# A first stage of one pass over tiles, rewritten as two passes over pairs of tiles by Strassen's form

## The chip, the cores and the metric

The kernel runs on one core of one Trainium2 chip. The metric is the device time of one execution in microseconds (us); lower is better. TensorE is called PE below, VectorE DVE, ScalarE ACT, GpSimd POOL, and SyncE, which here only issues DMAs, SP.

## What is computed

One layer of a transformer-like block on 2048 positions of width 1024, all float32:

```python
h = rms_norm(x, norm_mix_pre)
z = h @ w_in                      # 1024 -> q 512 | k 128 | v 128 | u 512 | v 512
q, k = apply_rope(q), apply_rope(k)
a_out = window_sink_attention(q, k, v, attn_sinks)   # 8 heads, 2 kv heads, chunks of 64
g_in = gelu(z[..., o3:])
s_out = spatial_gating(g_in[..., :512], g_in[..., 512:], ...)  # layer norm, 128x128 per group
mix = concat([rms_norm(a_out), rms_norm(s_out)]) @ w_out
x = x + rms_norm(mix)
x = x + rms_norm(swiglu(rms_norm(x), w_gate, w_up, w_down))
```

The change concerns the first product (`h @ w_in`) and what hangs on it: the gate branch (u, v, gelu, spatial gating), and q, k, v with the attention.

## The kernel before

A float32 product is made of three fast ones: each operand is split into a rounded part `_hi` (a copy on ACT, type fp32r) and a rest `_lo` (a subtraction on DVE), and `three` issues hi\*hi, hi\*lo and lo\*hi. The gain of the pre-norm is multiplied into the weights while they are split; the row factor `rstdx` is applied when the result is read.

There are four stages. **Stage one** loops over 16 tiles of 128 positions. For each, PE makes q, k, v into `ZA` (`z_qkv`: 24 matmuls of 512 columns and 24 of 256) and u, v of the gate branch into `ZB` (`z_columns`, 48 matmuls of 512 columns), plain products over 8 chunks of 128. Between them stand, in an order that is written out by hand, the transposes of q and k, the scores, the transposes of the probabilities, the spatial product (`sgu_w`) and the weighted sum of the values. The products for tile k+1 are issued while ACT and DVE do the softmax of tile k, so PE always has a long product between two short steps that wait. The result `mix` goes to DRAM (`mix_d`). **Stage two** (`tile2`) reads it back, multiplies by `w_out` (48 matmuls a tile), adds the residual, norms and stores. Its first two products begin in the last tile of stage one. **Stage three** (gate and up of the SwiGLU) and **stage four** (down) already use Strassen's form: of a 2x2 block product 7 block products are made in place of 8. For that the left and the right operand each need four sums, and the result needs chains of sums. In stage three `t_sums` on POOL makes the sums of the weights, `t_hi_parts` on ACT and `t_lo_parts` on DVE split them in three instructions, `copies` on ACT brings products 1 and 2 from PSUM, `chain`, `upper` and `lower` on DVE and `corner` on POOL put the quarters of the result together. Stages three and four are not touched.

Each engine works through its own list in order; a `wait_ge` at the head of a list holds everything behind it on that engine. All DMAs are issued by SP, also in order.

Of the kernel before, what the change touches and what calls it, by code (L numbers as in the profile page):

```python
# [5 lines left out]
F32 = mybir.dt.float32  # L6
# [6 lines left out]
P = 128  # L13
# [6 lines left out]
SW = 512  # L20
# [14 lines left out]
RAWS = 6  # L35
# [10 lines left out]
def build_kernel(nc, x, x_t, w_in, w_out, w_gu, w_dn, gain_in, gain_out, post_mix, pre_ffn,  # L46
                 post_ffn, sinks, ln_g, ln_b, sgu_wt, sgu_bt, rope, out):
    mix_d = nc.dram_tensor("mix_d", (SEQ, D), F32).ap()
    x1_d = nc.dram_tensor("x1_d", (SEQ, D), F32).ap()
# [12 lines left out]
    wq_hi = at("wq_hi", 90, [KD, QKV], F32R)  # L62
    wq_lo = at("wq_lo", 114, [KD, QKV], F32R)
    wg_hi = at("wg_hi", 138, [KD, 2 * SW], F32R)
    wg_lo = at("wg_lo", 170, [KD, 2 * SW], F32R)
    wraw = [at(f"wraw{i}", 10 + 4 * i if i < 4 else 48 + 4 * i, [2 * SW]) for i in range(RAWS)]
    ropeA = at("ropeA", 0, [AW + P])
    ropeB = at("ropeB", 2.5, [AW + P])
    qT = at("qT", 5, [AW])
    kA = [at(f"kA{i}", 7 + 0.5 * i, [P]) for i in range(2)]  # L70
    kB = at("kB", 8, [P])
    vA = [at(f"vA{i}", 8.5 + 0.5 * i, [P]) for i in range(2)]
    vB = at("vB", 9.5, [P])
    probs = at("probs", 10, [NH * P])
    probsT = at("probsT", 14, [NH * P])
    gel = at("gel", 18, [2 * SW])
    vhat = at("vhat", 22, [SW])
    vn1 = at("vn1", 24, [SW])
    vn = at("vn", 26, [SW])
    sB = at("sB", 28, [SW])  # L80
    aO = at("aO", 30, [AW])
    hT_hi = [at(f"hT_hi{i}", 32 + 4 * i, [D], F32R) for i in range(2)]
    hT_raw = [at(f"hT_raw{i}", 40 + 4 * i, [D]) for i in range(2)]
    hT_lo = [at(f"hT_lo{i}", 40 + 4 * i, [D], F32R) for i in range(2)]
    xt = [at(f"xt{i}", 48 + 4 * i, [D]) for i in range(2)]
    qrot = at("qrot", 60, [AW])
    krot = at("krot", 62, [P])
    mix = [at(f"mix{i}", 64 + 4 * i, [D]) for i in range(2)]
    cs = at("cs", 72, [TILES, 96])
    lng = at("lng", 78, [SW])  # L90
    lnb = at("lnb", 80, [SW])
    squares1 = at("squares1", 82, [D], BF16)


    wout_raw = [at(f"wout_raw{c}", 88 + 4 * c, [D]) for c in range(KD)]
    wout_hi = at("wout_hi", 120, [KD, D], F32R)
    wout_lo = at("wout_lo", 152, [KD, D], F32R)
# [48 lines left out]
    gcol_in, gcol_out = small("gcol_in", KD), small("gcol_out", KD)  # L146
# [3 lines left out]
    ssx, msx, rstdx = small("ssx", 2), small("msx", 2), small("rstdx", 2)  # L150
# [3 lines left out]
    st6, mv, varm, rstdv = small("st6", 6), small("mv", 2), small("varm", 1), small("rstdv", 1)  # L154
    ss2, ms2, rs2 = small("ss2", 2), small("ms2", 2), small("rs2", 2)
# [14 lines left out]
    DN = [T0[:, :], T1[:, :]]  # L170

# [8 lines left out]
    wraw_in = [sem(f"wraw_in{i}") for i in range(RAWS)]  # L180
    win_hi_done, win_split = sem("win_hi_done"), sem("win_split")
    x_in, hT_in, mix_out = pair("x_in"), pair("hT_in"), pair("mix_out")
    id_zero, pool_consts = sem("id_zero"), sem("pool_consts")
    ssx_done, msx_ready, rstdx_ready = sem("ssx_done"), sem("msx_ready"), sem("rstdx_ready")
    t_full, t_drained = pair("t_full"), pair("t_drained")
    h_hi_done, h_split, zqkv_full, zus_full = sem("h_hi_done"), sem("h_split"), sem("zqkv_full"), sem("zus_full")
    rope_mul, rot_done, v_done, k_done = sem("rope_mul"), sem("rot_done"), sem("v_done"), sem("k_done")
    gel_done, st6_done, mv_done, var_ready = sem("gel_done"), sem("st6_done"), sem("mv_done"), sem("var_ready")
    rstdv_ready, vhat_done, vn1_done, vn_ready = sem("rstdv_ready"), sem("vhat_done"), sem("vn1_done"), sem("vn_ready")
    s_full, masked, mraw_done = sem("s_full"), sem("masked"), sem("mraw_done")  # L190
    mtop_done, soft_ready, exp_done = sem("mtop_done"), sem("soft_ready"), sem("exp_done")
    dtot_done, rden_done, g_full, pv_done = sem("dtot_done"), sem("rden_done"), sem("g_full"), sem("pv_done")
    sB_done, aO_done, ss2_done, ms2_ready = sem("sB_done"), sem("aO_done"), sem("ss2_done"), sem("ms2_ready")
    rs2_ready, mix_done = sem("rs2_ready"), sem("mix_done")
# [47 lines left out]
    def use_q(k):  # L242
        return 2 * k

    def use_p(k):
        return 2 * k + 1

    def over_tiles(e, body):

        body(0, 0, 0, 0, True)
        body(0, 1, 1, 0, True)
        with e.Fori(1, TILES // 2 - 1) as j:
            for par in range(2):
# [12 lines left out]
    PIECES = [(c, wq_hi, wq_lo, slice(0, QKV)) for c in range(KD)] + \  # L268
             [(c, wg_hi, wg_lo, slice(QKV, WIN)) for c in range(KD)]

    def piece(i):
        c, hi, lo, w = PIECES[i]
        return c, w, wraw[i % RAWS][:, 0:w.stop - w.start], hi[:, c, :], lo[:, c, :]

    block = nc.Block()
    with block:

        @block.sync
        def _(e):
            e.dma_start(hT_raw[0][:, :], x_t[0, :, :]).then_inc(hT_in[0], 16)  # L280
            e.dma_start(gcol_in[:, :], gain_in).then_inc(gains_in, 16)
            for i in range(len(PIECES)):
                c, w, raw, hi, lo = piece(i)
                if i >= RAWS:
                    e.wait_ge(win_split, i + 1 - RAWS)
                e.dma_start(raw, w_in[chunk(c), w]).then_inc(wraw_in[i % RAWS], 16)
                if i == 3:
                    for m in range(2):
                        e.dma_start(xt[m][:, :], x[m * P:(m + 1) * P, :]).then_inc(x_in[m], 16)
                    e.dma_start(hT_raw[1][:, :], x_t[1, :, :]).then_inc(hT_in[1], 16)  # L290
                    e.dma_start(cs[:, 0:1, :], rope[:, 0:1, :]).then_inc(cs_in, 16)
            for dst, src in ((cs[:, 1:TILES, :], rope[:, 1:TILES, :]), (sgu_w[:, :, :], sgu_wt)):
                e.dma_start(dst, src).then_inc(consts, 16)
            for dst, src in ((sgub, sgu_bt), (sinkb, sinks), (lng, ln_g), (lnb, ln_b), (gcol_out, gain_out)):
                e.dma_start(dst[:, :], src).then_inc(consts, 16)
            for m in (2, 3):
                e.wait_ge(ssx_done, m - 1)
                e.dma_start(xt[m % 2][:, :], x[m * P:(m + 1) * P, :]).then_inc(x_in[m % 2], 16)

            def tile(k, par, more, ahead=True):  # L300
                if more:
                    e.wait_ge(ssx_done, k + 3)
                    e.dma_start(xt[par][:, :], x[rows(k + 4), :]).then_inc(x_in[par], 16)
                if ahead:
                    e.wait_ge(zus_full, k + 1)
                    e.dma_start(hT_raw[par][:, :], x_t[bass.ds(k + 2, 1), :, :].rearrange("t p n -> (t p) n"))\
                        .then_inc(hT_in[par], 16)
                e.wait_ge(mix_done, 2 * k + 2)
                e.dma_start(mix_d[rows(k), :], mix[par][:, :]).then_inc(mix_out[par], 16)

            with e.Fori(0, TILES // 2 - 2) as j:
                for par in range(2):
                    tile(j * 2 + par, par, True)
            for k in range(TILES - 4, TILES - 2):
                tile(k, k % 2, False)


            e.wait_ge(zqkv_full, TILES)
            for c in range(KD):
                e.dma_start(wout_raw[c][:, :], w_out[chunk(c), :]).then_inc(wout_in[c], 16)  # L320
            for p in range(2):
                e.wait_ge(mix_out[p], 16 * (TILES // 2 - 1))
                e.dma_start(mixin[p][:, :], mix_d[p * P:(p + 1) * P, :]).then_inc(mix_in[p], 16)
            tile(TILES - 2, 0, False, False)
            e.wait_ge(zus_full, TILES)
            for p in range(2):
                e.wait_ge(rot_done, 2 * TILES)
                e.wait_ge(t_full[1], use_q(TILES - 1) + 1)
                e.dma_start(xres[p][:, :], x[p * P:(p + 1) * P, :]).then_inc(xres_in[p], 16)
            e.dma_start(postm[:, :], post_mix).then_inc(posts, 16)  # L330
# [5 lines left out]
            def load_mix(k, par):  # L336
                e.wait_ge(mixT_full, 2 * k - 2)
                e.dma_start(mixin[par][:, :], mix_d[rows(k), :]).then_inc(mix_in[par], 16)
# [1139 lines left out]
```

## Time and profile before

| | us |
|---|---|
| median of 3 runs | 1917.43 (1917.12 to 1918.08) |
| profiled execution | 1919.53 |
| its span in the profile | 1917.7 |
| first matmul | 8.84 |
| gate product of the first tile starts | 23.31 |
| gate product of the last tile starts | 393.30 |
| first two products with `w_out` done | 441.46 |

The profiled execution is 2.1 us above the median; 1.8 us of it lie outside the span. The last line of the table is the end of stage one for this document: from there on both kernels do the same. A row of a timeline gives start, duration, engine, line and operation; the durations of matmuls overlap, so their pace is read from their starts.

### The profile page before, as it was taken

What the parts mean: (1) busy time and instruction counts of PE and PEld (TensorE: products, weight loads), DVE (VectorE), ACT (ScalarE), POOL (GpSimd) and SP (SyncE); (2) the same over time, 40 slices, a digit from 0 to 9 for tenths busy, and PEclk for the clock granted to TensorE, in tenths of its full rate; (3) what the DMA queues carried; (4) which work ended last, traced back from release to release, by engine and by line L of the source; (5) the groups of instructions that cost most, each with busy time, mean ns of one, the idle gap of its engine ahead of it and who ended that gap; (6) DMA issues with size and microseconds to landing.
All of it is one profiled execution on the core that took longest, in us unless ns stands there. A gap on an engine that the chain in (4) does not pass through costs nothing. (4 is left out here: it accounts for less than half of the span.)

```text
span 1917.7 us, 25255 instructions
## 1 busy us (share of the span) xinstructions
PE 1866.2 (97%) x9464; PEld 1545.9 (81%) x9464; DVE 1178.6 (61%) x1286; ACT 711.6 (37%) x1169; POOL 560.8 (29%) x406
## 2 busy tenths in 40 slices
PE   7999999989999899999999899999999899999998
PEld 5888888878888788888888688888887788888886
DVE  5444444464546877677767867677767546554564
ACT  6555555453335432323234333323333122222342
POOL 2222222220002444444444444444442000000243
PEclk9999999999999999999999999999999999999999
DMA  7111111044574434233326333233324853445665
GB/s 274 67 66 66 66 66 55 33 179 178 206 275 183 171 103 130 87 104 98 126 82 221 119 108 117 82 104 116 108 82 151 335 212 126 174 167 187 228 206 180
DMA packets 128966, 270.26 MB, mean 141 GB/s; under 512 B 5920, under 2 KB 84768, under 8 KB 119456
## 3 DMA queue, kind: packets, MB, share of 16 engines
q1 hardware_dynamic: 128928, 269.78, 40.3%
q8 instruction: 21, 0.34, 0.1%
q14 instruction: 17, 0.14, 0.0%
HBM read 189.54 MB, written 80.22 MB: 141 GB/s over the span
## 5 line engine op out<-in xcount | busy, mean ns | idle before, releaser
L1220 PE MATMUL T<-tb_hi,sb_hi 128*128 128x512 f32 x616 | 240.9, 391 | 7.1 <-DVE sb_lo L1133 7.1
L1221 PE MATMUL T<-tb_lo,sb_hi 128*128 128x512 f32 x616 | 240.2, 390 | 0.0
L1222 PE MATMUL T<-tb_hi,sb_lo 128*128 128x512 f32 x616 | 240.2, 390 | 0.0
L1018 DVE TENSOR_TENSOR t_lo<-t_raw,t_hi 128x1536 fp32r<-128x1536 f32 x132 | 223.8, 1749 | 0.0
L807 ACT ACTIVATE sb_hi<-sb_raw 128x1408 fp32r<-128x1408 f32 x56 | 77.4, 1381 | 299.1 <-PE T L1222 259.5
L571 POOL TENSOR_TENSOR v<-u,p 128x512 f32<-128x512 f32 x44 | 116.2, 2640 | 183.4 <-DVE u L1042 158.3
L1397 PE MATMUL T<-s_hi,t_hi 128*128 128x512 f32 x352 | 138.6, 394 | 6.4 <-DVE s_lo L1011 4.5
L555 POOL TENSOR_TENSOR t_raw<-t_raw 128x512 f32<-128x512 f32 x44 | 60.8, 1381 | 281.1 <-DMA t_raw<-w_gu 281.1
L1220 PEld LDWEIGHTS T<-tb_hi,sb_hi 128*128 128x128 f32 x616 | 116.0, 188 | 32.9 <-issue 8.2
L1399 PE MATMUL T<-s_hi,t_lo 128*128 128x512 f32 x352 | 138.4, 393 | 0.0
L1398 PE MATMUL T<-s_lo,t_hi 128*128 128x512 f32 x352 | 138.0, 392 | 0.0
L1397 PE MATMUL ZB<-s_hi,t_hi 128*128 128x512 f32 x352 | 136.9, 389 | 0.0
L1398 PE MATMUL ZB<-s_lo,t_hi 128*128 128x512 f32 x352 | 136.9, 389 | 0.0
L1399 PE MATMUL ZB<-s_hi,t_lo 128*128 128x512 f32 x352 | 136.9, 389 | 0.0
L1221 PEld LDWEIGHTS T<-tb_lo,sb_hi 128*128 128x128 f32 x616 | 116.1, 188 | 24.2
L1222 PEld LDWEIGHTS T<-tb_hi,sb_lo 128*128 128x128 f32 x616 | 115.9, 188 | 24.1
L1133 DVE TENSOR_TENSOR sb_lo<-sb_raw,sb_hi 128x1408 fp32r<-128x1408 f32 x56 | 96.2, 1718 | 51.5 <-ACT sb_hi L807 51.5
L756 ACT ACTIVATE th<-v 128x512 f32<-128x512 f32 x66 | 41.7, 632 | 218.1 <-POOL v L571 120.0
L595 POOL TENSOR_TENSOR rstdf<-msf,mhalf 128x1 f32<-128x1 f32 x16 | 14.5, 906 | 359.9 <-ACT msf L816 359.9
L1397 PE MATMUL ZA<-s_hi,t_hi 128*128 128x512 f32 x264 | 104.6, 396 | 4.9 <-DVE u L1042 2.7
L1220 PE MATMUL ZB<-wg_hi,hT_hi 128*128 128x512 f32 x256 | 103.1, 403 | 1.6 <-DVE wg_lo L967 1.6
L1398 PE MATMUL ZA<-s_lo,t_hi 128*128 128x512 f32 x264 | 104.1, 394 | 0.0
(194 smaller groups left out, 4522.4 us busy)
## 6 DMA issues: line engine op xcount, KB each, us to landing
t_raw<-w_gu SPq DMA_DIRECT2D x44, 1024.0 KB, 4.8
act_d<-ac SPq DMA_DIRECT2D x22, 1792.0 KB, 8.0
sb_raw<-act_d SPq DMA_DIRECT2D x56, 704.0 KB, 4.1
h_d<-quarters SPq DMA_DIRECT2D x8, 1792.0 KB, 6.6
s_raw<-h_d SPq DMA_DIRECT2D x14, 1024.0 KB, 8.1
tb_raw<-w_dn SPq DMA_DIRECT2D x6, 1536.0 KB, 6.3
hT_raw<-x_t SPq DMA_DIRECT2D x16, 512.0 KB, 3.2
xt<-x SPq DMA_DIRECT2D x16, 512.0 KB, 3.9
```

Of the source, the lines that this page charges most:

```text
L555: e.tensor_tensor(t[:, R3, :], t[:, B22, :], t[:, B12, :], ALU.subtract).then_inc(tsum_done, 1)
L571: e.tensor_tensor(v22[:, :], u3[:, :], p5[:, :], ALU.add).then_inc(v22_done, 1)
L756: e.activation(th[i][:, :], src, ACT.Tanh, scale=0.5).then_inc(th_done, 1)
L807: e.activation(sb_hi[it % 2][:, :, :], sb_raw[it % 2][:, :, :], ACT.Copy).then_inc(sb_hi_done, 1)
L1018: e.tensor_tensor(t_lo[u][:, first:end, :], t_raw[u][:, first:end, :], t_hi[u][:, first - 1:end - 1, :].bitcast(F32), ALU.subtract).then_i ...
L1133: e.tensor_tensor(sb_lo[it % 2][:, :, :], sb_raw[it % 2][:, :, :], sb_hi[it % 2][:, :, :].bitcast(F32), ALU.subtract).then_inc(sb_split, 1)
L1220: e.matmul(out_ap, lhi, rhi, start=start, stop=False)
L1221: e.matmul(out_ap, lhi, rlo, start=False, stop=False)
L1222: return e.matmul(out_ap, llo, rhi, start=False, stop=stop)
L1397: e.matmul(bank, hi, s_hi[i][:, :, w], start=i < 4 and k == 0, stop=False, skip_group_check=True)
L1398: e.matmul(bank, hi, s_lo[i][:, :, w], start=False, stop=False, skip_group_check=True)
L1399: ins = e.matmul(bank, lo, s_hi[i][:, :, w], start=False, stop=k == HK - 1, skip_group_check=True)
```

## The change

Stage one becomes two passes over 8 pairs of tiles. The first goes from the last pair (j = 0) to the first one (j = 7) and does the gate branch; the second goes from the first pair (p = 0) to the last and does q, k, v with the attention. Both use Strassen's form over the pair: 7 products of 12 matmuls, of 512 columns in pass one (`uv_product`) and of 384 in pass two (`qkv_product`).

The left operand comes as four quarters of x (`x_q`, 1024 KB a pair). DVE multiplies them by the gain (`scale_xq`, 128x2048), POOL makes four sums (`left_sums`), ACT and DVE split the seven operands (`left_hi`, `left_lo`). They are stored to DRAM (`hl_d`, twice 1792 KB a pair) and loaded again by pass two (`load_hl`). The right operands (weights) are summed and split once per pass: for pass one at the start, for pass two in the last iteration of pass one. The chains of sums are those of stage three, on DVE (`uv_u2`, `uv_u3`, `uv_upper`, `uv_lower`) and POOL (`bv22`). The normed half of the gate branch now goes through two instructions on DVE (`tn`, `vn`) where DVE made one and POOL two. Gelu no longer alternates with Exp on ACT. The first two products with `w_out` are spread between the attention steps of the last three tiles.

The diff, cut to its core:

```diff
+            def left_sums(j):
+                q = lb_raw[j % 2]
+                e.wait_ge(xq_scaled, j + 1)
+                e.tensor_tensor(q[:, 4, :], q[:, 0, :], q[:, 3, :], ALU.add).then_inc(lsum_done, 1)
+                e.wait_ge(lsum_done, 4 * j + 1)
+                e.tensor_tensor(q[:, 5, :], q[:, 4, :], q[:, 1, :], ALU.subtract).then_inc(lsum_done, 1)
+                e.tensor_tensor(q[:, 6, :], q[:, 1, :], q[:, 0, :], ALU.subtract).then_inc(lsum_done, 1)
+                e.wait_ge(lsum_done, 4 * j + 2)
+                e.tensor_tensor(q[:, 7, :], q[:, 2, :], q[:, 5, :], ALU.subtract).then_inc(lsum_done, 1)
...
+                if j + 1 == NP:
+                    e.wait_ge(w_in_loaded[B12], 32)
+                    e.wait_ge(w_in_loaded[B22], 32)
+                    e.wait_ge(in_done, 7 * j + 4)
+                    e.tensor_tensor(wq_raw[3][:, :, :], wq_in[:, B22, :, :], wq_in[:, B12, :, :],
+                                    ALU.subtract).then_inc(w_sum3, 1)
...
+            for j in range(NP):
+                ahead = j + 1 < NP
+                uv_copy(j, 0)
...
+                if ahead:
+                    stats_x(j + 1)
+                    left_hi(j + 1, 1)
+                    left_hi(j + 1, 2)
+                else:
+                    for i in range(1, 5):
+                        wq_hi_part(i)
+                gelus(j)
...
+            def left_lo(j, c):
+                b = j % 2
+                first, end = ((1, 4), (4, 6), (6, 8))[c]
+                if c == 0:
+                    e.wait_ge(lsum_done, 4 * j + 4)
...
+                if ahead:
+                    scale_xq(j + 1)
+                else:
+                    wq_lo_part(0)
+                if j:
+                    gate(j - 1, 0)
+                if ahead:
+                    left_lo(j + 1, 0)
+                else:
+                    wq_sum(R1)
+                uv_u2(j)
...
+                uv_u3(j)
+                if ahead:
+                    left_lo(j + 1, 1)
+                    left_lo(j + 1, 2)
+                norm_stats(j, 1)
+                normed(j, 1)
...
+                uv_upper(j)
+                norm_stats(j, 0)
+                uv_lower(j)
...
+                normed(j, 0)
...
+            def uv_product(j, i):
...
+                if i in (4, 5):
+                    e.wait_ge(in_copied, 2 * j + i - 3)
+                if i == 6:
+                    e.wait_ge(u3_first, j + 1)
...
+            def spatial(j, par):
+                n = 2 * j + 1 - par
...
+                e.wait_ge(vn_ready, n + 1)
+                if par:
+                    e.wait_ge(v21_first, j + 1)
...
+            for j in range(NP):
+                for i in range(7):
+                    uv_product(j, i)
+                    if j and i < 2:
+                        spatial(j - 1, 1 - i)
...
+            e.wait_ge(w_split, 7 + 7)
+            load_hl(1)
```

`in_done` counts products, `u3_first`, `v12_first`, `v21_first`, `v22_first` the parts of the result (`bu3`, `bv12`, `bv21`, `bv22`), `vn_ready` the normed halves, `w_split` the split weights, `lsum_done` the sums on POOL.

DVE, one tile of the kernel before, inside its loop (`hT_lo` is the split of the left operand, `st`, `mv`, `varm`, `vhat` the layer norm, `sB` the gate's result, `mix` what is stored):

```order
L851 TENSOR_TENSOR hT_lo_81<-hT_raw_79,hT_hi_77 128x1024
...
L904 BN_STATS st_191<-gel 128x6
L907 BN_AGGR mv<-st_191 128x2
L909 TENSOR_SCALAR varm<-mv 128x1
L913 TENSOR_SCALAR vhat<-gel,mv,rstdv 128x512
...
L934 SCALAR_TENSOR_TENSOR sB<-S,sgub,gel 128x128 x4
...
L945 TENSOR_SCALAR mix_87<-sB,rs_197 128x512
```

DVE, one iteration of pass one in the changed kernel (`lb_raw` the quarters and sums of the left operand, `lb_lo` their rests, `bu`, `bv` the chain, `tn`, `vn` the norm; the two halves of the norm read alike, the first is shown whole):

```order
L1123 SCALAR_TENSOR_TENSOR sB_94<-ZA,sgub,gu_88 128x128 x4
L1077 TENSOR_TENSOR lb_raw_70<-lb_raw_70,gq 128x2048
L1123 SCALAR_TENSOR_TENSOR sB_93<-ZA,sgub,gu_87 128x128 x4
L1087 TENSOR_TENSOR lb_lo_72<-lb_raw_70,lb_hi_74 128x1536
L1159 TENSOR_TENSOR bu_82<-S,bp_80 128x512
L1131 TENSOR_SCALAR sB_94<-sB_94,rsB 128x512
L1131 TENSOR_SCALAR sB_93<-sB_93,rsB 128x512
L1166 TENSOR_TENSOR bu_83<-S,bu_82 128x512
L1087 TENSOR_TENSOR lb_lo_72<-lb_raw_70,lb_hi_74 128x1024 x2
L1137 BN_STATS st_261<-bv_86 128x6
L1139 BN_AGGR mv<-st_261 128x2
L1141 TENSOR_SCALAR varm<-mv 128x1
```

The list went from one split of 1024 elements a tile to a scaling of 2048 and splits of 3584 a pair, with four sums of PSUM banks, and the split of the next pair stands ahead of this pair's `bu_83`.

POOL, the same iteration in the changed kernel (`rsB`, `rstdx`, `rstdv` are powers of a column or two, `bv_86` is `bv22`):

```order
L529 TENSOR_TENSOR lb_raw_70<-lb_raw_70 128x512
L531 TENSOR_TENSOR lb_raw_70<-lb_raw_70 128x512
L532 TENSOR_TENSOR lb_raw_70<-lb_raw_70 128x512
L534 TENSOR_TENSOR lb_raw_70<-lb_raw_70 128x512
L524 TENSOR_TENSOR rsB<-msB,mhalf 128x2
L524 TENSOR_TENSOR rstdx<-msx,mhalf 128x2
L565 TENSOR_TENSOR bv_86<-bu_83,bp_81 128x512
L524 TENSOR_TENSOR rstdv<-varm,mhalf 128x1 x2
```

All of these are new there but the powers; the sums of the next pair stand ahead of this pair's `bv_86`.

DVE at the start of the changed kernel, up to the first weights (`wu_b` and `wu_raw` are loaded or summed weights, `wu_lo` their rests):

```order
L1077 TENSOR_TENSOR lb_raw_70<-lb_raw_70,gq 128x2048
L1096 TENSOR_TENSOR wu_lo_56<-wu_b_97,wu_hi_63 128x2048
L1103 TENSOR_TENSOR wu_raw_50<-wu_b_98,wu_b_97 128x2048
L1107 TENSOR_TENSOR wu_raw_51<-wu_raw_54,wu_raw_50 128x2048
L1087 TENSOR_TENSOR lb_lo_72<-lb_raw_70,lb_hi_74 128x1536
```

Before the first product stood one split of `hT_raw` (1024 elements) and one of 768 elements; now the scaling, a split and two sums of 2048 each and a split of 1536 stand there.

## Rows read from the trace of the kernel before

**Rows 1.** The page: span, and busy time of each engine
```profile
span 1917.7 us, 25255 instructions
PE 1866.2 (97%) x9464; PEld 1545.9 (81%) x9464; DVE 1178.6 (61%) x1286; ACT 711.6 (37%) x1169; POOL 560.8 (29%) x406
```

**Rows 2.** Windows: a start, tiles 1 to 14, a cold stretch; busy, clock, DMA
```profile
8.00:12.00 4.00, 3.16 (x9) 2.72 (x10) 3.60 (x4) 2.37 (x3) 0.00 (x0) 1.00 1.03 417
...
44.00:393.40 349.40, 348.19 (x2610) 292.50 (x2608) 166.30 (x356) 176.71 (x478) 90.40 (x99) 1.00 0.17 59
...
1076.00:1080.00 4.00, 3.91 (x10) 3.17 (x11) 4.00 (x3) 1.12 (x2) 2.66 (x1) 0.57 1.03 291
```

**Rows 3.** Timeline of PE: the first matmul, one tile, the last tile's start
```profile
8.84 0.77 PE L1220 MATMUL ZA<-wq_hi,hT_hi 128*128 128x512 f32 x1 [8.84 <-DVE wq_lo L967]
...
202.77 0.39 PE L1222 MATMUL ZB<-wg_hi,hT_lo 128*128 128x512 f32 x1
...
203.65 0.47 PE L1220 MATMUL ZB<-wg_hi,hT_hi 128*128 128x512 f32 x1
...
208.99 0.39 PE L1222 MATMUL ZB<-wg_hi,hT_lo 128*128 128x512 f32 x1
...
210.34 0.50 PE L1220 MATMUL ZA<-wq_hi,hT_hi 128*128 128x512 f32 x1
...
216.07 0.28 PE L1221 MATMUL ZA<-wq_lo,hT_hi 128*128 128x256 f32 x1
...
218.71 0.28 PE L1222 MATMUL ZA<-wq_hi,hT_lo 128*128 128x256 f32 x1
218.83 1.04 PE L1313 MATMUL T<-ident,probs 128*128 128x128 f32 x8
219.70 1.06 PE L1320 MATMUL S<-vn,sgu_w 128*128 128x128 f32 x8
220.84 0.27 PE L1329 MATMUL S<-vA,probsT 128*64 128x64 f32 x1
...
221.92 0.50 PE L1220 MATMUL ZB<-wg_hi,hT_hi 128*128 128x512 f32 x1
...
393.30 0.50 PE L1220 MATMUL ZB<-wg_hi,hT_hi 128*128 128x512 f32 x1
...
441.46 0.71 PE L1347 MATMUL S<-ident,h2n 128*128 128x128 f32 x5
```

**Rows 4.** Timeline of ACT: product 1 of two neighbouring halves in stage three
```profile
902.35 0.60 ACT L749 ACTIVATE p<-T 128x512 f32<-128x512 f32 x1 [12.45 <-PE T L1399]
...
921.39 0.60 ACT L749 ACTIVATE p<-ZB 128x512 f32<-128x512 f32 x1 [0.39 <-PE ZB L1399]
```

**Rows 5.** Timeline of DVE: wide subtractions, without and with POOL beside them
```profile
614.55 4.49 DVE L1011 TENSOR_TENSOR s_lo<-s_raw,s_hi 128x2048 fp32r<-128x2048 f32 x2
618.96 4.02 DVE L1018 TENSOR_TENSOR t_lo<-t_raw,t_hi 128x1536 fp32r<-128x1536 f32 x3
...
911.28 5.11 DVE L1018 TENSOR_TENSOR t_lo<-t_raw,t_hi 128x1536 fp32r<-128x1536 f32 x3
```

**Rows 6.** Timeline of POOL: the corner beside them, and one of the four sums
```profile
911.59 2.58 POOL L571 TENSOR_TENSOR v<-u,p 128x512 f32<-128x512 f32 x1 [3.40 <-DVE u L1042]
...
1038.13 1.29 POOL L558 TENSOR_TENSOR t_raw<-t_raw 128x512 f32<-128x512 f32 x1
```

**Rows 7.** Timeline of DVE: the layer norm and the gate's result
```profile
212.09 0.69 DVE L904 BATCH_NORM_STATS2 st<-gel 128x6 f32<-128x512 f32 x1
...
213.16 0.15 DVE L909 TENSOR_SCALAR varm<-mv 128x1 f32<-128x1 f32 x1
...
222.22 1.12 DVE L934 SCALAR_TENSOR_TENSOR sB<-S,sgub,gel 128x128 f32<-128x128 f32 x4
```

**Rows 8.** DMA issues: KB each, median us from issue to landing
```profile
t_raw<-w_gu SPq DMA_DIRECT2D x44, 1024.0 KB, 4.8
...
h_d<-quarters SPq DMA_DIRECT2D x8, 1792.0 KB, 6.6
```

More of the change, by code:

```diff
@@ L84, in build_kernel @@
[L84 to L96, printed above, removed]
@@ L300, in tile @@
[L300 to L309, printed above, removed]
@@ L311, in _ @@
[L311 to L323, printed above, removed]
@@ L871, in rope_products, with keys @@
                                            op0=ALU.mult, op1=ALU.mult).then_inc(rope_mul, 1)
-            def tile(j, par, before, last, ahead):
-                k = 2 * j + par
-                if not last:
-                    h_lo(k + 1, 1 - par)
-                e.wait_ge(t_full[1], use_q(k) + 1)
+            def keys(k):
+                par = k % 2
+                e.wait_ge(k_full, k + 1)
+                if k:
+                    e.wait_ge(s_full, k)
                 e.tensor_copy(kB[:, :], T1[:, 0:P]).then_inc(k_done, 1)
@@ new lines, in spatial @@
+            def spatial(j, par):
+                n = 2 * j + 1 - par
+                if n == 0:
+                    e.wait_ge(pool_consts, 4)
+                e.wait_ge(vn_ready, n + 1)
+                if par:
+                    e.wait_ge(v21_first, j + 1)
+                bank = GU[j % 2][2 + par]
+                for g in range(SG):
+                    ins = e.matmul(bank[:, chunk(g)], sgu_w[:, g, :], vn[par][:, chunk(g)], start=True, stop=True)
+                ins.then_inc(g_full, 1)
@@ L1295, in tile @@
                 for i in range(PAIRS):
-                    for half, keys in enumerate((kA[par], kB)):
+                    for half, window in enumerate((kA[k % 2], kB)):
                         for kv in range(KVH):
@@ new lines, in out_units @@
+            def out_units(k, first, end):
+                par = k % 2
+                if first == 0:
+                    e.wait_ge(mixT_split, 2 * k + 2)
+                    if k == 0:
+                        e.wait_ge(z11_done, NP)
+                        e.wait_ge(v12_first, NP + NP)
+                    if k == 1:
+                        e.wait_ge(u2_first, NP + NP)
+                        e.wait_ge(v21_first, NP + NP)
+                    if k >= 2:
+                        e.wait_ge(y_done, k - 1)
+                for unit in range(first, end):
+                    c, a = unit // 2, unit % 2
+                    w = slice(a * 512, (a + 1) * 512)
+                    if k == 0 and a == 0:
+                        e.wait_ge(wout_split, c + 1)
+                    ins = three(M[par][:, a, :], mixT_hi[par][:, chunk(c)], mixT_lo[par][:, chunk(c)],
+                                wout_hi[c][:, w], wout_lo[c][:, w], c == 0, c == KD - 1)
+                if end == 2 * KD:
+                    ins.then_inc(mm2_full, 1)
@@ new lines, in _ @@
+            for i in range(7):
+                qkv_product(0, i)
+                if i < 2:
+                    spatial(NP - 1, 1 - i)
+            for j in range(NP - 1):
+                p = j + 1
+                qkv_product(p, 0)
+                turn_qk(2 * j)
+                if j:
+                    turn_probs(2 * j - 1)
+                qkv_product(p, 1, range(0, 2))
+                scores(2 * j)
+                qkv_product(p, 1, range(2, 4))
+                qkv_product(p, 2)
+                if j:
+                    weighted(2 * j - 1)
+                qkv_product(p, 3)
+                turn_qk(2 * j + 1)
+                qkv_product(p, 4, range(0, 2))
+                turn_probs(2 * j)
+                qkv_product(p, 4, range(2, 4))
+                scores(2 * j + 1)
+                if p == NP - 1:
+                    mix_transposes(0)
+                qkv_product(p, 5)
+                qkv_product(p, 6)
+                weighted(2 * j)
@@ new lines, in _ @@
+            out_units(0, 0, 3)
+            turn_qk(TILES - 2)
+            turn_probs(TILES - 3)
+            out_units(0, 3, 5)
+            scores(TILES - 2)
+            out_units(0, 5, 9)
+            weighted(TILES - 3)
+            out_units(0, 9, 12)
+            turn_qk(TILES - 1)
+            out_units(0, 12, 16)
+            mix_transposes(1)
+            turn_probs(TILES - 2)
+            out_units(1, 0, 2)
+            scores(TILES - 1)
+            weighted(TILES - 2)
+            out_units(1, 2, 11)
```

1336 lines of the change are left out of this document (869 added, 467 removed).

## The prediction

> **What bounds the kernel now.** I read the page first: PE is busy for 97% of the span [rows 1], so only what shortens PE's list, or makes it wait, can move the time. Then the windows: from 44 to 393 us, fourteen tiles, PE is busy for 348.19 of 349.40 us, while DVE works 166, ACT 177 and POOL 90 of them [rows 2]. Stage one is bound by PE, and the others have slack of half their time. The timeline of PE gives its prices. A matmul of 512 columns takes 0.2267 us: two neighbouring halves of stage three, 84 matmuls each, start 19.04 apart [rows 4]. One of 256 takes 0.120 (22 of them from 216.07 to 218.71). A tile takes (393.30-221.92)/7 = 24.48; less 72 x 0.2267 and 24 x 0.120 this leaves 5.28 for its small steps: transposes of q and k (203.65-202.77, less one matmul, 0.65), scores (1.12), transposes of the probabilities (0.87), spatial product (1.14), weighted sum (1.08), and some 0.4 for the switches [rows 3]. Stage one with the two first products of `w_out` ends at 441.46. Its content on PE is 16 x 24.48 + 96 x 0.2267 + 3 for the transposes of `mix` = 416.5; so 25 us are waits, 8.84 of them ahead of the first matmul.
>
> **What PE's list saves.** Pass one, a pair: 84 x 0.2267 = 19.04, and two spatial products at 1.14 + 0.2 for the switch: 21.7. Pass two, a pair: 84 matmuls of 384 columns, a size that the trace doesn't have; between 0.120 and 0.2267 I take the middle, 0.1733, which makes 14.56 (bounds 10.1 and 19.0; the two paces lie on a line through nearly zero, so the middle is good to some hundredths). With it go the small steps of two tiles without the spatial ones, 2 x 4.14, and some 0.5 for two more switches: 23.3. In all 8 x 21.7 + 8 x 23.3 + 24.8 = 385. The list is 31 us shorter. The Trainium skill (TensorE: Matmul & The Clock Gate, "Wait — 56ns, not 53.3ns?") gives a warm matmul its columns at 2.4 GHz and about 2.5 ns; by that 384 columns would take 0.1625 and pass two would be 7 us shorter in all. The rows at 512 columns lie 5% above what it gives, so the sum stays with the rows.
>
> **What DVE and POOL get: the steady pair of pass one.** Here the gain is lost. Prices on DVE, start to start: 0.61 for 512 elements, 1.13 for 1024, 1.67 for 1536 (4.02 for the three parts of a split), 2.2 for 2048 (4.49 for two) [rows 5], 1.05 for the four parts of the gate's result, 1.22 from `bn_stats` to the end of `varm` [rows 7]. A sum of 512 on POOL takes 1.29 and its four follow one another in 5.4 [rows 6]. And the two engines exclude each other when both have two inputs in SBUF: the same split takes 4.02 alone and 5.11 with the corner beside it, which takes 2.58 in place of 1.29 [rows 5, 6].
>
> I walk once through DVE's list from y, the moment at which `uv_lower` of the pair before is done. PE has waited for it (`v21_first`), and makes the spatial product: the gate's first half can start at y+1.45 (the second half of the norm fits before it) and ends at y+2.5. Scaling, 2.2: y+4.7. Only now can POOL begin the sums, done at y+10.2; DVE makes the second gate (1.05) and then stands for 4.4 us, since `left_lo` wants all four sums. Split of 1536: y+11.9. `uv_u2` 0.61, and two products with `rsB` (0.8), which wait for POOL's two powers, themselves locked out by that split (some 0.6): y+13.9. `uv_u3`: y+14.5. The two splits of 1024 with the corner between them: 1.13 + 1.3 + 1.13, y+18.1. The norm's first half: 1.22 + 0.61, some 0.6 for the power on POOL behind it, 0.61: y+21.1. `uv_upper` 0.61, 0.8 for the gelu that it feeds on ACT, second half of the norm 1.83, `uv_lower` 0.61: y+25.0, and some 0.3 for semaphores. The loop is **25.3**, against PE's 21.7: PE stands 3.6 us in each pair, in front of the spatial product. So pass one is DVE's, with DVE busy for only 17. Bounds: 22.8 if no lock cost anything, 27 if each met twice. The loads don't set it: `x_q` is issued as the pair before ends and lands 4.8 later [rows 8], before its scaling.
>
> **The start.** Loads run at 417 GB/s [rows 2], so a megabyte lands every 2.5 to 3 us: `x_q` near 5.8, the quarters of the weights near 8.6, 11.4, 14.2 and 17. DVE has scaling, seven splits and three sums of 2048 and a split of the left operand in three parts: 11 x 2.2 + 4 = 28 us, and the lock adds a sum on POOL of four times 1.29 (5.2) and one of 1.3; it starts at 5.9 and waits 3.5 for the first rounded weights. The first matmul starts near 26.7 in place of 8.84 [rows 3], the weights are done at 44. Product 7 waits for `uv_u3`, behind the scaling (2.2), the sums (5.4), a split (1.67) and two sums of the next pair: 54.5. The first pair ends at **57.2**. Its `uv_lower` comes 10.5 after `uv_u3`, so y is 7.9 for the second pair, which takes 7.9 + 19.2 = **27.1**; pairs 3 to 7 take 5 x 25.3 = **126.5**.
>
> **From pass one to pass two.** In the last iteration the weights of pass two take the place of the left splits. Counted from its start: `uv_u3` at 22, the corner at 23.3, then on POOL a difference of 1536 (three times 1.29, 3.9): 27.2. ACT's list has the rounding of this and of the next weight (1.5 each) ahead of all gelus, so the norm can start only at 31; with two splits of 1536 in between, `uv_lower` ends near 40. PE is through with the pair at 25, has one product of pass two (2.1) to do, and stands 12 us in front of the spatial product. The rest of that pair of products ends near 55. The next one needs `hl_d`, whose load waits for the last split of the weights (near 50; it lands where `wq_in` lay): twice 1792 KB, 11 us at 417 GB/s with the landing (13.2 if they ran one after the other at 6.6 [rows 8]). It starts near **62.5**; its content would have been 39.
>
> **Pass two and the end.** A tile's chain through the scores (scores 1.1, maxima 1.7, exponentials 2.9, transposes 0.9, copy 0.7, semaphores) is under 8 us and comes twice in 23.3; DVE has some 15, ACT 14 and POOL 6 us of work. I charge nothing, and the cover is the seven products: 21.1 for the pair that has no tile behind it, 6 x 23.4, and a transposition: **162.6**. The end: 96 matmuls, the small steps of two and a half tiles, transposes of `mix`, and 1 for waits: **35.5**.
>
> **The sum.** 57.2 + 27.1 + 126.5 + 62.5 + 162.6 + 35.5 = 471.4 in place of 441.5: 30 longer. Seen otherwise: 31 less on PE, 61 more in waits (start about 23, pass one 23, the passage 23, less what stood at the old end). The later stages are the same. The profiled span of 1917.7 becomes 1948; the median lies 0.3 below the span: **1947**. From one measurement to the next this kernel differs by less than 0.2%, 3.8 us, which I take as the bound of "same".
>
> **Rivals.**
> *The queues as walked* (0.62): 1935 to 1960. The parts are good to 1 us a pair in pass one (7), 4 each at the start and the passage, 1 a pair in pass two.
> *Some of the waits don't come* (0.18): DVE's order bites less than I walk, say 22.8 a pair for want of locks (-18 over seven pairs) and some of the passage: 1916 to 1933. For it speaks that in stage three the same chain leaves PE without waits; against it, that there the sums on POOL are made long before DVE wants them, here never.
> *PE stays the bound* (0.12), the rival on the other side: if a pair costs DVE less than 21.7 and the passage is covered, the 31 us come back in full: 1886, and half of them with the start as walked, 1903. It decides at 21.7; DVE's own work is 17, and the 4.4 for the sums would have to vanish. The order of DVE's list speaks against it: nothing stands between the second gate and the split.
> *It is worse* (0.08): each wait of PE is followed by a cold stretch (clock 0.57 in a window after such a wait [rows 2]), which DVE's loop hides in pass one but nothing hides at the start and in the passage; or pass two waits 2 us a pair for a list on ACT or DVE: 1962 to 1975.
>
> **How the numbers follow.** The first case gives 1947. From 1920 to 1963 lie all of it and most of the second, some 8 in 10; its own range is 1935 to 1960. Faster, below 1913.6: the third case, 0.12. Same: 0.06, out of the second. Slower: 0.82.
>
> **What would show it.** In the profile after: first matmul near 27; starts of product 1 in pass one 25 us apart, with PE idle 3 to 4 us released by DVE's `bv` (line 1176) ahead of the spatial product; DVE idle 4 to 5 us a pair released by POOL (line 534) ahead of line 1087; a wait of 12 us at the passage and one of 7 released by the DMA of `hl_d`; starts in pass two 23.4 apart. I am wrong if pairs of pass one are 22 us apart, or if ACT makes its gelus ahead of the weights.

## The result, and the profile after

The changed kernel takes 1966.05 us (median of 4 runs, 1964.69 to 1970.17), the kernel before 1917.76 in the same comparison: ratio 1.0251, 95% interval 1.0239 to 1.0264. It is slower, as forecast, and 3 us above the upper end of the range of 1920 to 1963.

The page of the changed kernel, to be held against [rows 1]. Its profiled execution took 1964.88 us.

```profile
span 1963.0 us, 24683 instructions
...
PE 1841.8 (94%) x9272; PEld 1538.7 (78%) x9272; DVE 1273.7 (65%) x1386; ACT 714.2 (36%) x1201; POOL 605.7 (31%) x424
```

PE has 24 us less to do, and the span is 45.3 longer: the saving is there, and some 70 us of waits eat it. The timeline of PE gives the borders of the parts of the sum; in brackets stands the idle time before the row, and what ended it.

```profile
26.35 0.77 PE L1696 MATMUL T<-wu_hi,lb_hi 128*128 128x512 f32 x1 [26.35 <-DVE lb_lo L1087]
...
48.28 0.77 PE L1696 MATMUL T<-wu_hi,lb_hi 128*128 128x512 f32 x1 [5.15 <-ACT bp L713]
...
59.81 0.63 PE L1696 MATMUL ZB<-wu_hi,lb_hi 128*128 128x512 f32 x1
...
65.62 1.13 PE L1710 MATMUL ZA<-vn,sgu_w 128*128 128x128 f32 x8 [2.65 <-DVE bv L1176]
...
83.88 0.39 PE L1696 MATMUL T<-wu_hi,lb_hi 128*128 128x512 f32 x1
...
91.23 2.05 PE L1710 MATMUL S<-vn,sgu_w 128*128 128x128 f32 x8 [4.47 <-DVE bv L1176]
...
212.19 0.39 PE L1696 MATMUL ZB<-wu_hi,lb_hi 128*128 128x512 f32 x1
...
217.06 1.75 PE L1710 MATMUL ZA<-vn,sgu_w 128*128 128x128 f32 x8 [1.99 <-DVE bv L1176]
...
250.80 2.04 PE L1710 MATMUL S<-vn,sgu_w 128*128 128x128 f32 x8 [11.61 <-DVE bv L1176]
...
273.79 0.69 PE L1745 MATMUL ZA<-wq_hi,lb_hi 128*128 128x384 f32 x1 [6.52 <-DMA lb_lo<-hl_d]
...
435.77 0.47 PE L1669 MATMUL ZA<-wout_hi,mixT_hi 128*128 128x512 f32 x1 [1.55 <-DVE z L1269]
...
444.00 1.08 PE L1759 MATMUL T<-ident,qrot 128*128 128x128 f32 x4 [5.92 <-issue]
...
488.30 1.04 PE L1896 MATMUL S<-ident,h2n 128*128 128x128 f32 x8
```

Each term of the forecast sum beside what these rows give (the pairs start at 59.81, 83.88 and, the last of pass one, 212.19):

| part | forecast | measured |
|---|---|---|
| first pair | 57.2 | 59.8 |
| second pair | 27.1 | 24.1 |
| pairs 3 to 7 | 126.5 | 128.3 |
| last of pass one to second pair of pass two | 62.5 | 61.6 |
| pass two | 162.6 | 162.0 |
| end, up to the first transposes of stage two | 35.5 | **52.5** |
| sum | 471.4 | 488.3 |

Five of six terms are good to 3 us and cancel; the end is 17.0 us too short, the whole miss of 16.9 at this border. The waits inside it, beside the one of 5.92 above:

```profile
454.01 0.50 PE L1669 MATMUL ZA<-wout_hi,mixT_hi 128*128 128x512 f32 x1 [1.13 <-DVE wout_lo L1351]
...
460.51 0.50 PE L1669 MATMUL ZA<-wout_hi,mixT_hi 128*128 128x512 f32 x1 [1.64 <-DVE wout_lo L1351]
...
463.10 0.50 PE L1669 MATMUL ZA<-wout_hi,mixT_hi 128*128 128x512 f32 x1 [0.92 <-DVE wout_lo L1351]
...
469.19 0.50 PE L1669 MATMUL ZB<-wout_hi,mixT_hi 128*128 128x512 f32 x1 [2.69 <-DVE mixT_lo L1359]
...
484.17 0.24 PE L1800 MATMUL T<-vA,probsT 128*64 128x64 f32 x1 [1.08 <-ACT probsT L837]
```

What follows the border takes 1474.7 us, before 1476.2 (1917.7 less 441.46). The windows of the end show both halves of its excess, idle PE and a low clock (columns as in [rows 2]):

```profile
444.00:452.00 8.00, 8.00 (x57) 6.55 (x58) 4.54 (x11) 4.17 (x9) 2.24 (x3) 0.66 0.00 1
...
468.00:476.00 8.00, 6.81 (x77) 5.26 (x78) 3.59 (x7) 1.67 (x8) 0.55 (x1) 0.79 0.90 310
...
435.00:488.00 53.00, 38.86 (x304) 30.44 (x305) 27.88 (x51) 27.40 (x88) 6.67 (x10) 0.90 0.24 80
```

The longest wait of the end, 5.92 us ahead of the turn of q and k of tile 14, is one for several semaphores, and the profile writes "issue" where it names none. The timeline of DVE shows what was late:

```profile
439.15 1.28 DVE L1351 SCALAR_TENSOR_TENSOR wout_lo<-wout_raw,gcol_out,wout_hi 128x1024 fp32r<-128x1024 f32 x1 [1.27 <-ACT wout_hi L852]
442.01 1.28 DVE L1351 SCALAR_TENSOR_TENSOR wout_lo<-wout_raw,gcol_out,wout_hi 128x1024 fp32r<-128x1024 f32 x1 [1.58 <-ACT wout_hi L852]
443.21 0.68 DVE L1338 TENSOR_TENSOR aO<-T,rden 128x512 f32<-128x512 f32 x1
```

and that of ACT why:

```profile
437.93 1.18 ACT L852 ACTIVATE wout_hi<-wout_raw,gcol_out 128x1024 fp32r<-128x1024 f32 x1
440.83 1.15 ACT L852 ACTIVATE wout_hi<-wout_raw,gcol_out 128x1024 fp32r<-128x1024 f32 x1 [1.71 <-DVE wout_lo L1351]
```

The turn (the transposes of q and k) overwrites the bank from which DVE still has to read the output of tile 12 (`aO`, 443.21; it ends at 443.89, and the turn starts at 444.00). That reading stands in DVE's list behind two splits of `w_out`, these behind ACT's, the first of ACT's behind eight exponentials, and the second waits for DVE's first, since an odd part waits for the split before it. A relay of four steps lies ahead of an instruction of 0.7 us.

### The profile page after: what moved, and what is told of

Its sections match the earlier page's. It is cut to its first block and busy times, and to the rows that moved or that the text cites. A ratio compares the mean times of both kernels' runs of the same rounds, so it can differ in the third digit from the quotient of the medians.

```text
span 1963.0 us, 24683 instructions
## 1 busy us (share of the span) xinstructions
PE 1841.8 (94%) x9272; PEld 1538.7 (78%) x9272; DVE 1273.7 (65%) x1386; ACT 714.2 (36%) x1201; POOL 605.7 (31%) x424
## 3 DMA queue, kind: packets, MB, share of 16 engines
q1 hardware_dynamic: 132816, 321.17, 46.1%
## 5 line engine op out<-in xcount | busy, mean ns | idle before, releaser
L1670 PEld LDWEIGHTS T<-tb_lo,sb_hi 128*128 128x128 f32 x616 | 116.1, 188 | 24.1
L1671 PEld LDWEIGHTS T<-tb_hi,sb_lo 128*128 128x128 f32 x616 | 116.1, 188 | 24.1
L1933 PE MATMUL ZA<-s_hi,t_lo 128*128 128x512 f32 x264 | 103.5, 392 | 0.0
```

Source lines behind the costliest of these rows:

```text
L1670: e.matmul(out_ap, lhi, rlo, start=False, stop=False)
L1671: return e.matmul(out_ap, llo, rhi, start=False, stop=stop)
L1933: ins = e.matmul(bank, lo, s_hi[i][:, :, w], start=False, stop=k == HK - 1, skip_group_check=True)
```

## Experiments

Each run was measured beside the kernel before. Ratios are to that kernel, as 1.0251 is for the changed one.

**1. The end: two splits moved.** In DVE's list:

```diff
-                if j == NP - 2:
-                    wout_lo_part(2)
-                    wout_lo_part(3)
...
                 keys(2 * j)
+                if last:
+                    wout_lo_part(2)
+                    wout_lo_part(3)
```

> Edit: DVE's lower parts 2 and 3 of w_out leave their place behind the last upper-half work of pair 6 and stand behind the keys of tile 14, so that the output of tile 12 no longer stands behind them. Theory (the end was under-priced because DVE's list puts w_out's splits, which wait for ACT, ahead of the last tile outputs): the wait of 5.9 us ahead of the query turn of tile 14 goes, with it the cold stretch behind it (about 3 us), and some of it comes back at the w_out products: 1958 to 1961 us, ratio to the changed kernel 0.996 to 0.9975. Rival (the tail is bound by the count of operations on DVE, so the place of two of them does not matter): the wait moves to the next w_out product, 1965 to 1967 us.

1963.72 us, 1.0239 (1.0222 to 1.0256). The wait of 5.92 became one of 1.09, and 2.54 came back at the next scores. From the first product with `w_out` to the end: 438.04 to 486.41, 48.4 us where it was 52.5. (The unchanged end of runs 2 to 6 took 50.9 to 53.9, so the size of this gain is good to some 2 us.) In time only half of that shows, since the part before it took 2.3 us longer in the profiled execution; why pass one is so restless, runs 3 to 6 show. The time lies between the range of the theory and that of the rival: the theory holds for this wait, and its time came only in part.

**2. The passage: ACT's gelus ahead of its weights, and DVE's norm ahead of its own.**

```diff
-                    for i in range(1, 5):
+                    for i in range(1, 3):
                         wq_hi_part(i)
                 gelus(j)
+            wq_hi_part(3)
+            wq_hi_part(4)
...
+                normed(j, 0)
                 if not ahead:
                     wq_lo_part(3)
-                normed(j, 0)
```

> Edit: at the passage between the passes ACT does the gelus of the last pair ahead of the upper parts 3 and 4 of w_q, and DVE normalises the last pair's first tile ahead of the lower part 3. Theory (the wait of 11.6 us ahead of the last spatial product is DVE waiting for gelus that stand behind w_q's splits in ACT's list): that wait shrinks to 2 to 4 us, and 8 to 10 us go unless the w_q products of the first pair of pass two then wait for the splits moved back: 1956 to 1959 us. Rival (the passage is bound by the load and the split of w_q, so what is saved ahead of the spatial product is lost behind it): 1964 to 1966 us.

1960.13 us, 1.0217 (1.02 to 1.0234). The wait of 11.61 fell to 6.70, and from the spatial product before it to the second pair of pass two it took 53.1 us (219.35 to 272.40) where it took 56.7. The wait shrank by 4.9 us, the stretch by 3.7, where the theory had 8 to 10: the order in the lists is one cause of the wait, not the only one. What ACT's list and what DVE's brought of it isn't shown, since both were changed.

**3 and 4. Pass one: DVE's list, and POOL's sums.** The first scales x ahead of the gate; the second makes the four sums on DVE, right behind the scaling.

```diff
-                if j:
-                    gate(j - 1, 1)
                 if ahead:
                     scale_xq(j + 1)
+                if j:
+                    gate(j - 1, 1)
```

> Edit: in pass one DVE scales the next pair's x ahead of the second gate of the pair before. Theory (the loop of 25.3 us runs over DVE's list: scaled x, POOL's four sums, the lower parts of the sums, and DVE waits 4.4 us in it for POOL): scaled x comes 1.9 us earlier, the wait for POOL shrinks by as much, loop 23.2 to 23.8 us, 7 pairs: 1951 to 1956 us. Rival (the wait only moves, since DVE has the same operations and POOL's sums are slowed by DVE's gate beside them): loop 25.0 to 25.4 us, 1964 to 1967 us.

> Edit: the four left sums of a pair (A11+A22, A21+A22 and so on) are done by DVE right behind the scaling of x, not by POOL. Theory (DVE's wait for POOL's sums, 4.4 us a pair, is in the loop; on DVE the sums cost about 2 us a pair more of its own time): loop 22.5 to 23.5 us a pair, first pair 2 to 4 us earlier, in all 1945 to 1954 us. Rival (DVE's own work is the bound and the wait for POOL only fills time in which it waits for PE or ACT anyway): loop 25 to 27 us, 1964 to 1975 us.

1964.08 us, 1.0238, and 1963.51 us, 1.0236 (1.0219 to 1.0254). Both theories failed on the loop. With x scaled earlier, the spatial products stand 25.4 apart (65.93 to 218.26, six pairs), in the changed kernel 25.2 (65.62 to 217.06). With the sums on DVE the first comes 3.9 us earlier (61.77), and then they stand 25.7 apart (61.77 to 215.75, six pairs), in turn some 23.3 and 28.0. DVE's list is the same in each of these pairs, so it gives no reason to alternate, and I looked for another cause. Timelines of ACT, DVE and PE in a long pair of the second kernel:

```profile
99.43 1.06 ACT L691 ACTIVATE squares<-xs 128x1024 bf16<-128x1024 f32 x1 [3.90 <-DMA xs<-x]
...
102.98 3.27 DVE L1084 TENSOR_TENSOR lb_lo<-lb_raw,lb_hi 128x1024 fp32r<-128x1024 f32 x2 [4.70 <-ACT lb_hi L674]
...
113.01 2.04 PE L1709 MATMUL ZA<-vn,sgu_w 128*128 128x128 f32 x8 [6.90 <-DVE bv L1173]
```

ACT waits for x, loaded for the row sums, and behind that wait stands the rounding of the next pair, which DVE wants. In the changed kernel it is the same; its table of DMA issues in pass one has

```profile
hl_d<-lb_hi SPq DMA_DIRECT2D x6, 1792.0 KB, 10.4
hl_d<-lb_lo SPq DMA_DIRECT2D x6, 1792.0 KB, 15.5
...
xs<-x SPq DMA_DIRECT2D x12, 512.0 KB, 16.2
```

and its waits there ACT's for this load (19.4 us) beside DVE's for POOL and for ACT:

```profile
ACT squares L704 <- DMA xs<-x: 19.4, 5, 5.7
...
DVE lb_lo L1087 <- POOL lb_raw L534: 20.1, 6, 3.8
DVE lb_lo L1087 <- ACT lb_hi L687: 8.1, 4, 3.1
```

Each 512 KB take 16.2 us and are issued by SP behind 3.5 MB of stores, and the stores themselves stand in SP's list behind a load (the next `x_q`) that waits for the pair before to end. Whether that place makes them late, run 5 tests.

**5 and 6. The load ahead of the stores, alone and with the sums on DVE.**

```diff
                 if j + 1 < NP:
-                    store_hl(j)
                     load_xs(j + 1)
+                    store_hl(j)
```

> Edit: in pass one the load of x for the row sums (512 KB a pair) is issued ahead of the two stores of the rounded left operands (3.5 MB a pair), not behind them. In the runs before this one ACT waited for this load 4 or 5 times in pass one, up to 5.7 us, and the rounding of the left sums and DVE's lower parts stood behind that wait; scaling x earlier or making the sums on DVE left the loop at 25.6 to 26. Theory (the loop is set by two chains of nearly one length, DVE's list with POOL's sums and this load behind the stores, so that relief of one alone gains little): alone it takes away the pairs of 26.7 us, loop 24.4 to 24.9, 1959 to 1963 us. Rival (the load is late only because the pair is long anyway): no wait for it, but loop 25.2 to 25.4, 1965 to 1967 us.

(Of x there are two loads of 512 KB a pair.)

> Edit: the load of x for the row sums ahead of the stores, and the left sums on DVE. Theory (two chains): now both are relieved, the waits ahead of the spatial products of 6.6 to 7.0 us in every second pair go, loop 23.0 to 23.6 us, 7 pairs, and the start as in the run with the sums alone: 1944 to 1951 us. Rival (DVE's own list is the bound once it makes the sums, the load only marks it): loop 25.0 to 25.7, 1962 to 1965 us.

1956.93 us, 1.0198 (1.0181 to 1.0215), and 1944.35 us, 1.0136 (1.0119 to 1.0153). The load now lands in 7.1 and 7.3 us, and in neither kernel does ACT wait for it in pass one; in the table of run 5:

```profile
xs<-x SPq DMA_DIRECT2D x12, 512.0 KB, 7.1
```

PE's timeline in the two kernels:

```profile
113.15 1.13 PE L1710 MATMUL ZA<-vn,sgu_w 128*128 128x128 f32 x8 [2.51 <-DVE bv L1176]
...
136.82 1.13 PE L1710 MATMUL S<-vn,sgu_w 128*128 128x128 f32 x8 [2.54 <-DVE bv L1176]
```

```profile
106.11 1.13 PE L1709 MATMUL ZA<-vn,sgu_w 128*128 128x128 f32 x8 [1.38 <-DVE bv L1173]
...
128.62 1.13 PE L1709 MATMUL S<-vn,sgu_w 128*128 128x128 f32 x8 [1.36 <-DVE bv L1173]
```

The loop is 23.7 and 22.5 us, in both shorter than expected, and no longer alternates. Against the ratio 1.0251 the load alone brings 0.0053, the sums alone 0.0015, both 0.0115: more than the sum, as two chains of nearly one length would give. The Trainium skill ("DMA: Bandwidth & Descriptors", section "Queues, rings and completion order") says that descriptors of one ring are taken in ring order though their completions are not ordered; the runs agree with the first half, 16.2 us behind the stores and 7.1 ahead of them.

**7. The end again.** The move of run 1, and ACT's odd parts no longer wait for DVE; DVE waits for itself instead:

```diff
             def wout_hi_part(c):
...
-                if c % 2:
-                    e.wait_ge(wout_split, c)
...
             def wout_lo_part(c):
                 e.wait_ge(wout_hi_done, c + 1)
+                if c % 2:
+                    e.wait_ge(wout_split, c)
```

> Edit: at the end of pass two, DVE's lower parts 2 and 3 of w_out stand behind the keys of tile 14 as in the first run, and the odd upper parts on ACT no longer wait for the lower part before them (DVE's odd lower parts wait in its place, for the part before them on their own engine). Theory (the end is long because of w_out's splits: each pair is a relay ACT, DVE, ACT, DVE, and the w_out products wait for its last member, 0.5 to 1.6 us each, as do the tile steps between them): from the first w_out product to the first transposes of the second stage 44 to 47 us, where the changed kernel took 52.5 and the first run 48.4 or so; 1956 to 1961 us. Rival (it waits on the products of the last pair, after which alone the weights' room is free, and on the chain of tile 15): 48 to 50 us as in the first run, 1962 to 1965 us.

1960.89 us, 1.0218 (1.0201 to 1.0236). The end took 45.6 us (439.11 to 484.67), as expected and 2.8 less than in run 1: of the 17 us that were too long, the order and the relay held some 7.

**8. All together.**

> Edit: all that has been tried and seen to shorten a stretch, in one kernel: the load of x ahead of the stores, the left sums on DVE, the gelus ahead of the later upper parts of w_q, and the tail's two edits. If the stretches are independent: loop 23.2 in place of 25.3 (14 us), start 2 to 4, passage 4 to 6, end 4 to 8: 1936 to 1943 us, ratio to the kernel before 1.010 to 1.013. If DVE's list stays the bound of pass one: 1948 to 1956 us. Neither brings it below the kernel before, since the start (first matmul at about 24.5 in place of 8.84), the load of the stored operands (6.5) and the rest of the passage stay.

1931.38 us, 1.0064 (1.0048 to 1.0081), 5 us below the expected range: the loop is 22.5, the end 46.1.

**9. Start, passage and end once more.** On top of that, POOL's sum of 2048 at the start (`wu_raw[3]`) and its difference of 1536 at the passage (`wq_raw[3]`) go into DVE's list. DVE makes part 2 of `w_q` behind the norms and part 4 of `w_out` ahead of the maxima, ACT part 6 of `w_out` ahead of the exponentials. In ACT's gelus and in PE's end:

```diff
+                if j + 1 == NP:
+                    wq_hi_part(3)
+                    wq_hi_part(4)
                 e.wait_ge(v12_first, j + 1)
...
             turn_qk(TILES - 1)
-            out_units(0, 12, 16)
-            mix_transposes(1)
             turn_probs(TILES - 2)
-            out_units(1, 0, 2)
+            out_units(0, 12, 14)
+            mix_transposes(1)
+            out_units(0, 14, 16)
             scores(TILES - 1)
+            out_units(1, 0, 2)
```

> Edit, on top of the run with all edits (1931.4 us): at the start the last sum of 2048 of w_uv is DVE's, not POOL's (in that run DVE's own sum beside it took 6.58 us in place of 2.3); at the passage ACT rounds w_q's parts 3 to 5 in the gaps between the gelus, DVE makes POOL's difference of 1536, and the lower part 2 stands behind the norms; at the end the lower part 4 of w_out stands ahead of the maxima of tile 14, the probabilities of tile 14 are turned ahead of the last w_out products of tile 0, and mix of tile 1 two units earlier. Theory (each stretch is bound by the order of DVE's and ACT's lists, which these edits shorten): first matmul near 20.5 in place of 25.0 and the spatial product of pair one 2 us earlier; wait ahead of the last spatial product 7.0 to 3.5 to 5, wait for the stored operands 6.8 to 4 to 6; from the first w_out product to the first transposes of stage two 46.1 to 41 to 44: in all 1919 to 1925 us, ratio to the kernel before 1.000 to 1.004. Rival (the waits only move to the next product, since the sum of DVE's work at each place stays): 1927 to 1932 us.

1926.38 us, 1.0040 (1.0026 to 1.0054), between the two. The first matmul came at 20.79, and the end took 40.1 us (407.40 to 447.51); its window says what the list of the end costs when little is waited for:

```profile
407.00:447.00 40.00, 34.62 (x304) 26.88 (x303) 27.20 (x49) 26.59 (x87) 8.24 (x10) 1.00 0.30 103
```

34.6 us of work at full clock, where the forecast had 34.5. At the passage the spatial product waited 5.27 in place of 7.01, but the stored operands 6.75 as before: spatial product and load moved together.

**10. The load's source first, and half a norm between two steps.** In pass one DVE's `uv_upper` goes between the two parts of the first norm; at the passage the lower parts 4 to 6 of `w_q`, whose sources lie where `hl_d` is loaded to, go first, ahead of the gates too, and SP waits for five parts, not seven. PE's waits for the weights follow the new order, and `qkv_u3` of the first pair goes ahead of `mix_B`:

```diff
-                normed(j, 1)
                 uv_upper(j)
+                normed(j, 1)
...
                 if not ahead:
-                    wq_lo_part(2)
-                    wq_lo_part(3)
+                    for i in (4, 5, 6, 2, 3):
+                        wq_lo_part(i)
```

> Edit, on top of the run before (1926.4 us): in pass one DVE forms the upper half of the next gelu's operand between the two parts of the first norm, where it stood 0.45 us for POOL's power and 0.79 us for ACT's gelu; at the passage DVE makes the lower parts 4 to 6 of w_q (whose sources lie where the stored operands are loaded to) ahead of parts 2 and 3 and of the gates, so that the load starts 6 us earlier. Theory (pass one is still DVE's loop, 22.5 us with PE waiting 1.37 in each pair; the load of the stored operands waits for DVE's list): loop 21.3 to 21.6, wait for the load 6.75 to 1 to 3: in all 1911 to 1917 us, ratio 0.996 to 1.000, so at or just below the kernel before. Rival (PE's own list is the bound at 22.5 less the switches, and the load is slow, not late): 1922 to 1926 us.

**1908.82 us** (1908.27 to 1910.38), ratio **0.9955** (0.9941 to 0.9968): the first version that is faster than the kernel before, and faster than expected. Its page and PE's timeline:

```profile
span 1906.8 us, 24686 instructions
...
PE 1830.6 (96%) x9272; PEld 1527.9 (80%) x9272; DVE 1295.2 (68%) x1420; ACT 712.9 (37%) x1201; POOL 548.3 (29%) x390
```

```profile
20.77 0.77 PE L1692 MATMUL T<-wu_hi,lb_hi 128*128 128x512 f32 x1 [20.77 <-DVE lb_lo L1078]
...
144.13 1.13 PE L1706 MATMUL ZA<-vn,sgu_w 128*128 128x128 f32 x8 [0.17 <-DVE bv L1167]
...
165.46 1.13 PE L1706 MATMUL S<-vn,sgu_w 128*128 128x128 f32 x8 [0.16 <-DVE bv L1167]
...
212.95 2.05 PE L1706 MATMUL S<-vn,sgu_w 128*128 128x128 f32 x8 [4.86 <-DVE bv L1167]
...
390.01 0.47 PE L1665 MATMUL ZA<-wout_hi,mixT_hi 128*128 128x512 f32 x1 [0.33 <-DVE z L1265]
```

Pairs of pass one are 21.3 apart and PE hardly waits: here pass one is at last PE's, near the 21.7 of the forecast's list. The load is issued at 218.50 (233.42 in run 9), and its wait is gone. Which of the edits at the passage brought how much isn't shown: they were made together.

## Why the forecast was right, and where it was wrong

**Direction: right; mechanism: right in the main.** PE's work shrank (in run 10, with few waits, by 36 us: 1866.2 in [rows 1], 1830.6 there), and a larger sum of waits took its place. First matmul forecast 26.7, measured 26.35; wait of 12 us at the passage, measured 11.61; of 7 for the stored operands, 6.52; pass two without charge, 162.6 against 162.0. (Its pairs stand 22.8 apart, not 23.4; its first pair, 22.6 for 21.1, and a wait of 1.55 at its end make up for that.) The pace of 384 columns, taken as 0.1733, is in the changed kernel's rows:

```profile
429.85 0.33 PE L1745 MATMUL ZA<-wq_hi,lb_hi 128*128 128x384 f32 x1
430.37 0.33 PE L1745 MATMUL ZA<-wq_hi,lb_hi 128*128 128x384 f32 x1
```

Three matmuls lie between these starts (the rows of the other two lines are not shown): 0.52 / 3 = 0.173. The estimate of 0.1625 from the Trainium skill ("TensorE: Matmul & The Clock Gate", section "Wait — 56ns, not 53.3ns?") is not what this kernel runs at.

**The step that failed: "The end: ... and 1 for waits: 35.5."** The content was right (34.6 in run 9), the waits were 13.4, and PE was slow after them. The waits: 5.92 for tile 12's output behind the splits, 3.7 for DVE's lower parts of `w_out`, 2.7 for `mixT_lo`, 1.1 for the last probabilities. What is left of 52.5 is 4.5 us, and the windows of 8 us at clock 0.66 and 0.79 lose 8 x 0.34 + 8 x 0.21 = 4.4. Pass one, the start and the passage had been walked queue by queue; the end had been counted on PE alone, though the change spreads eight splits and two products of `w_out` over the last three tiles. Runs 1, 7 and 9 took 4, 7 and 12 us out of it by order and one moved wait.

**A step that was wrong and didn't show: "The loads don't set it."** It looked at `x_q` only. The load of x for the row sums, which the change puts behind 3.5 MB of stores, held ACT up in five pairs, by up to 5.7 us. DVE's list with POOL's sums is worth 23.7 us a pair (run 5), not the 25.3 that were walked: DVE waits for POOL 3.3 a pair (19.9 in six), not 4.4. With the late load it was 25.2 to 25.7 in the changed kernel. Two errors of 1.5 us a pair cancelled by luck, and the term looked good for the wrong reason; runs 3 and 4 brought it to light. The first pair has such a fault too: a wait of 5.15 us for ACT's copy `bp` (48.28) that the walk doesn't have; the two pairs at the start miss by +2.6 and -3.0 and cancel.

**The last microseconds.** The forecast took the median 0.3 below the span; here the profiled execution was at the low end of its runs, and the median lies 3.1 above the span. So 15 of the 19 us between 1947 and 1966 are in the span, the rest in this.

**The rivals.** That it would be worse (0.08) came true in size. Of its two reasons one is there, cold stretches after waits with nothing to hide them, but they hold 4.4 of the 17.0 us, and at the end, where it didn't look. "Each wait" was too much: after the waits of 4.2 to 5.5 us ahead of a spatial product in pass one the next one came 5.3 us later, after those of 2.65, 1.87 and 1.91 us 3.7 later, and yet after one of 1.99 (217.06) again 5.3. "PE stays the bound" was said to need DVE's 4.4 us for the sums to vanish; run 10 gets there by making the sums on DVE, by the place of the load and by order, and gives 1909, not the 1886 of a start and a passage without waits.

## What to carry to other kernels

Walk every stretch where the order is new through all queues, and the end of a stage above all: counting one engine's list there gives its floor, not its time. A small load that stands behind large stores in one queue can hold whatever is queued behind its reader; look in the DMA table for a transfer whose landing time doesn't fit its size. Where a loop alternates between two lengths, or where shortening the supposed bound leaves it unchanged, look for a second chain of the same length, and relieve both in one kernel before giving either up.

## What the runs showed of the hardware

That DVE and POOL exclude each other with two inputs in SBUF was known from [rows 5, 6]; how unevenly was not. The waiting engine can be passed over by several instructions in a row. In the changed kernel a power on POOL, which in run 8 took 0.70 us at its second place, beside a DVE sum that reads PSUM, lasted from 37.08 to 46.7, while DVE made three splits and a scaling back to back, none of them longer than alone, and the sums of the next pair stood behind it:

```profile
37.08 9.63 POOL L524 TENSOR_TENSOR rstdx<-msx,mhalf 128x2 f32<-128x2 f32 x1 [14.65 <-ACT msx L707]
```

```profile
37.25 6.68 DVE L1096 TENSOR_TENSOR wu_lo<-wu_raw,wu_hi 128x2048 fp32r<-128x2048 f32 x3
43.86 2.27 DVE L1077 TENSOR_TENSOR lb_raw<-lb_raw,gq 128x2048 f32<-128x2048 f32 x1
```

The other way round a sum of 2048 on DVE took 6.43 us beside a POOL sum of the same size, 2.28 alone. The Trainium skill ("SBUF — State Buffer", section "Who interferes with whom") says that a DVE `tensor_tensor` with both inputs in SBUF contends with what GpSimd reads, and, of DVE's two-port modes, that whoever issues first has the shared pair for the whole instruction. That fits a single meeting; it doesn't say who is next, and here the power of 128x2 lost four times in a row.
